# Strassen's scheme for the full down projections of a two-layer hybrid encoder

## What is computed

```
h = rmsnorm(x, g_ffn)
z = dwconv3(h @ w_up)                 # 1024 -> 5632 channels, centred convolution of width 3
x = x + (silu(z_gate) * z_val) @ w_down      # 2816 -> 1024 channels
```

## Time and profile before

| what | value |
|---|---|
| median of 3 runs | 1104.07 us (1103.85 to 1104.14) |
| profiled execution, span from first to last instruction | 1102.4 us |
| what lies around the span, against the median | 1.7 us |
| PE busy | 1092.6 us, 99% |
| PEld busy | 905.8 us, 82% |
| DVE / ACT / POOL busy | 531.0 / 484.7 / 464.8 us |
| granted TensorE clock | 0.999 of full speed |

### The profile page before, as it was taken

The page is one execution under the profiler, slowest core; times in us unless marked ns, Lnnn a source line. Parts: engine busy times, 40 slices in busy tenths (PEclk is TensorE's granted clock), DMA queues, the critical chain, the costliest instruction groups (busy, mean ns, idle before and its releaser), DMA issues.

```text
span 1102.4 us, 16315 instructions
## 1 busy us (share of the span) xinstructions
PE 1092.6 (99%) x5328; PEld 905.8 (82%) x5328; DVE 531.0 (48%) x816; ACT 484.7 (44%) x656; POOL 464.8 (42%) x202
## 2 busy tenths in 40 slices
PE   9999999999999999999999999999999999999997
PEld 7788888888888888888878888888888888888886
DVE  5726755655215551255536368456541355314545
ACT  7835444454225441344557344346432454313451
POOL 5334234344534443544634332435444444444450
PEclk9999999999999999999999999999999999999999
DMA  8222223232222222222522212222332322232222
GB/s 301 93 96 78 68 76 105 78 109 100 96 95 94 97 96 95 96 96 97 180 97 81 91 63 74 95 77 96 115 95 76 115 96 95 79 117 91 96 77 78
DMA packets 33607, 108.79 MB, mean 99 GB/s; under 512 B 3984, under 2 KB 6800, under 8 KB 33552
## 3 DMA queue, kind: packets, MB, share of 16 engines
q1 hardware_dynamic: 32848, 107.03, 29.2%
q10 hardware_dynamic: 704, 1.07, 0.3%
HBM read 105.98 MB, written 2.10 MB: 98 GB/s over the span
## 4 chain that ended last, share of the span: by engine, by line
PE 97%; DVE 1%; DMA 1%; ACT 0%; POOL 0%; SPq 0%; issue 0%; DVEq 0%
PE acc L1044 28%; PE acc L1045 28%; PE acc L1046 28%; PE acc L1170 3%; PE acc L1171 3%; PE acc L1172 3%; PE side L1140 1%; PE side L1258 1%; PE side L1242 1%; DMA x<-xT 1%; PE side L1248 1%; PE side L1221 1%; DVE arena L1019 1%; PE side L1201 1%; PE acc L1132 0%; PE acc L1121 0%
## 5 line engine op out<-in xcount | busy, mean ns | idle before, releaser
L339 POOL TENSOR_TENSOR w_lo<-w_raw,w_hi 128x1024 fp32r<-128x1024 f32 x188 | 453.4, 2416 | 600.6 <-ACT w_hi L348 600.6
L1044 PE MATMUL acc<-xg_hi,w_hi 128*128 128x512 f32 x864 | 338.8, 392 | 0.0
L1045 PE MATMUL acc<-xg_lo,w_hi 128*128 128x512 f32 x864 | 336.3, 389 | 0.0
L1046 PE MATMUL acc<-xg_hi,w_lo 128*128 128x512 f32 x864 | 336.2, 389 | 0.0
L348 ACT ACTIVATE w_hi<-w_raw 128x1024 fp32r<-128x1024 f32 x190 | 200.0, 1057 | 255.2 <-PE acc L1046 219.2
L1044 PEld LDWEIGHTS acc<-xg_hi,w_hi 128*128 128x128 f32 x864 | 162.2, 188 | 35.8 <-issue 2.0
L1046 PEld LDWEIGHTS acc<-xg_hi,w_lo 128*128 128x128 f32 x864 | 162.2, 188 | 33.9
L1045 PEld LDWEIGHTS acc<-xg_lo,w_hi 128*128 128x128 f32 x864 | 162.2, 188 | 33.5 <-issue 0.5
L1044 PE MATMUL acc<-feat_hi,w_hi 128*128 128x512 f32 (+1 forms) x492 | 188.9, 384 | 0.0
L1045 PE MATMUL acc<-feat_lo,w_hi 128*128 128x512 f32 (+1 forms) x492 | 188.8, 384 | 0.0
L1046 PE MATMUL acc<-feat_hi,w_lo 128*128 128x512 f32 (+1 forms) x492 | 188.8, 384 | 0.0
(11 more groups left out here) (131 smaller groups left out, 803.2 us busy)
## 6 DMA issues: line engine op xcount, KB each, us to landing
w_raw<-slabs SPq DMA_DIRECT2D x190, 512.0 KB, 3.3
outT<-arena SPq DMA_DIRECT2D x7, 256.0 KB, 2.3
ln_sb<-ln_gb SPq DMA_DIRECT2D x2, 512.0 KB, 7.7
w_raw<-slabs SPq DMA_DIRECT2D x4, 128.0 KB, 4.6
x<-xT ACTq DMA_DIRECT2D x2, 256.0 KB, 4.6
x<-xT SPq DMA_DIRECT2D x2, 256.0 KB, 5.9
x<-xT ACTq DMA_DIRECT2D x1, 512.0 KB, 7.2
w_raw<-slabs SPq DMA_DIRECT2D x2, 256.0 KB, 6.9
```

Of the source, the lines that this page charges most:

```text
L339: pool.tensor_tensor(w_lo[:, w], w_raw[:, w], w_hi[:, w].bitcast(F32), ALU.subtract).then_inc(lo_done, 1)
L1044: pe.matmul(out, wh, ah, start=first, stop=False)
L1045: pe.matmul(out, wh, al, start=False, stop=False)
L1046: return pe.matmul(out, wl, ah, start=False, stop=last)
```

## The change

In the full parts, each quad of four down slabs (eight input tiles, four output tiles) is computed as a 2x2 by 2x2 block product with seven unit products in place of eight. The blocks of the weights are output tiles even/odd by input tiles even/odd (four slabs `raw(0)` to `raw(3)`, arranged anew on the host by `quad_major`); the blocks of the features are even/odd tiles by first/second half of the tokens (`H = 256`). A unit is 24 matmuls of 256 columns for two output tiles side by side in one bank: 4 pairs x 2 output tiles x 3 products. Below, U1 to U7 are the seven units of the first quad of a part and V1 to V7 those of the second, in PE's order; U3 is made in two halves, U3a and U3b.

```diff
+                def unit(bank, slot_of, pairs, moving, first):
+                    for k in pairs:
+                        for r in range(2):
+                            a = slot_of * SLAB + r * (SLAB // 2) + k * P
+                            xh, xl = moving(k)
+                            out = acc[bank][:, r * H:(r + 1) * H]
+                            pe.matmul(out, w_hi[:, a:a + P], xh, start=(first and k == 0 and r == 0), stop=False,
+                                      skip_group_check=True)
+                            pe.matmul(out, w_hi[:, a:a + P], xl, start=False, stop=False, skip_group_check=True)
+                            last = pe.matmul(out, w_lo[:, a:a + P], xh, start=False, stop=(k == KP - 1),
+                                             skip_group_check=True)
+                    return last
...
+                    pe.wait_ge(lo_sum, 3 * (n // 2) + 1)
+                    pe.wait_ge(y_ready, ys + 1)
+                    pe.wait_ge(feat_ready, feats + KT - 1)
+                    unit(0, 0, every_pair, b11, True).then_inc(unit_done, 1)
+                    pe.wait_ge(lo_sum, 3 * (n // 2) + 2)
+                    pe.wait_ge(y_ready, ys + 2)
+                    pe.wait_ge(t_ready, stages + 2 * KP - 1)
+                    unit(1, 1, every_pair, t1, True).then_inc(unit_done, 1)
+                    pe.wait_ge(lo_sum, 3 * (n // 2) + 3)
+                    pe.wait_ge(y_ready, ys + 3)
+                    unit(2, 3, range(0, 2), b21, True)
+                    pe.wait_ge(lo_done, L * NS + slab + 1 + RING)
+                    pe.wait_ge(unit_added, 3 * n + 1)
+                    unit(0, 2, range(0, 3), t2, False)
+                    pe.wait_ge(t_ready, stages + 2 * KP)
+                    unit(0, 2, range(3, 4), t2, False).then_inc(unit_done, 1)
+                    pe.wait_ge(lo_done, L * NS + slab + 3 + RING)
+                    pe.wait_ge(unit_added, 3 * n + 2)
+                    pe.wait_ge(feat_ready, feats + KT)
+                    unit(1, 1, every_pair, b22, False).then_inc(unit_done, 1)
...
```

DVE, in the stages of the full parts: the sums of the features (T1 to T4, in the arena), and in the last stage of a part also the four sums of the weights of the first quad, between the steps of the stage:

```diff
+                    scale(0)
+                    taps(0, 0)
+                    if sums is not None:
+                        sums(1)
+                        sums(2)
+                    scale(1)
+                    taps(0, 1)
+                    gate(0)
+                    if sums is not None:
+                        sums(4)
+                        sums(3)
+                    scale(2)
+                    dve.wait_ge(feat_hi_done, L * NF + tile + (KT + 1))
+                    dve.tensor_tensor(lo(0, H), gated[0][:, 0:H], hi(0, H).bitcast(F32), ALU.subtract)...
+                    dve.wait_ge(even_copied, stage + 1)
+                    dve.tensor_tensor(t1, gated[0][:, H:S], even_copy, ALU.subtract).then_inc(t_done, 1)
+                    taps(1, 0)
+                    dve.wait_ge(t_hi_done, stage * 2 + 1)
+                    dve.tensor_tensor(lo(H, H), t1, hi(H, H).bitcast(F32), ALU.subtract).then_inc(t_ready, 1)
+                    scale(3)
+                    taps(1, 1)
+                    gate(1)
+                    ... t2, t3, t4 ...
+                    if added is not None:
+                        added()
+                    ... lo(S, S) of the odd tile, then t_lo[:, t_at] (768 columns) ...
...
+                            dve.tensor_tensor(sum_s1, raw(1), raw(3), ALU.add).then_inc(sum_done, 1)
...
+                    make = sums_of(part, 1)
+                    make(1)
+                    low(0, raw(0), 1)
+                    add_unit(0, 0, 0, 2, 7 * n + 6, x_done, 3 * n + 1)
+                    make(2)
+                    low(1, sum_s1, 2)
+                    make(4)
+                    make(3)
+                    add_unit(0, 1, 0, 0, 7 * n + 7, x_done)
+                    low(3, raw(2), 3)
+                    add_unit(1, 0, 0, 3, 7 * n + 8, unit_added)
```

Fourteen additions of 512 columns (`add_unit`) take the place of the eight of a part. ACT makes a high part for each of the seven weight operands (14 in place of 8 a part) and in each stage a copy of the even half, T1's high part and the 768 columns of T2 to T4; its list for the first quad is, behind all of the last stage:

```diff
+                    act.wait_ge(t_done, stage * 2 + 2)
+                    on_its_own(act)
+                    act.activation(odd, gated[1], ACT.Copy).then_inc(feat_hi_done, 1)
+                    act.activation(t_of, t_raw[:, H:4 * H], ACT.Copy).then_inc(t_hi_done, 1)
...
+                def last_units(n, slab):
+                    act.wait_ge(unit_done, 7 * n + 1)
+                    act.wait_ge(sum_done, 4 * n + 4)
+                    unit_hi(0, raw(1), hi_done)
+                    act.wait_ge(unit_done, 7 * n + 2)
+                    unit_hi(1, sum_s4, hi_done)
```

POOL makes all seven low parts of the first quad and four of the second; DVE makes the other three (`low` above):

```diff
+            def low_quad(L, part, g):
+                n, slab = quad_at(L, part, g)
+                if g == 0:
+                    pool.wait_ge(hi_sum, 3 * n + 1)
+                    low(0, raw(0)).then_inc(lo_sum, 1)
+                    pool.wait_ge(hi_sum, 3 * n + 2)
+                    low(1, sum_s1).then_inc(lo_sum, 1)
+                else:
+                    pool.wait_ge(lo_sum_vector, 3 * (n // 2) + 1)
+                pool.wait_ge(hi_done, L * NS + slab + 1)
+                pool.wait_ge(sum_done, 4 * n + 4)
+                low(2, sum_s2[:, :]).then_inc(lo_done, 1)
+                if g == 0:
+                    pool.wait_ge(hi_sum, 3 * n + 3)
+                    low(3, raw(2)).then_inc(lo_sum, 1)
+                pool.wait_ge(hi_done, L * NS + slab + 2)
+                low(0, raw(1)).then_inc(lo_done, 1)
+                if g:
+                    pool.wait_ge(lo_sum_vector, 3 * (n // 2) + 3)
+                pool.wait_ge(hi_done, L * NS + slab + 3)
+                low(1, sum_s4).then_inc(lo_done, 1)
+                pool.wait_ge(hi_done, L * NS + slab + 4)
+                low(2, raw(3)).then_inc(lo_done, 1)
```

More of the change, by code:

```diff
@@ L148, in encoder @@
         z = [slot(i) for i in range(4)]
+        sum_s1, sum_s4 = slot(4, 2), slot(6, 2)
+        t_raw, even_copy = slot(20, 2), slot(22)[:, 0:H]
         acc = [ctx.enter_context(nc.psum_tensor(f"acc{i}", [P, S], F32)) for i in range(RING)]
@@ L334, in _, with low_slabs @@
                                    ALU.subtract).then_inc(lo_done, 1)
[L335 to L340, removed]
+            def low_slabs(L, first, end):
+                with pool.Fori(L * (NS // RING) + first // RING, L * (NS // RING) + end // RING) as q:
+                    for j in range(RING):
+                        pool.wait_ge(hi_done, q * RING + (j + 1))
+                        low(j, raw(j)).then_inc(lo_done, 1)
@@ L343, in _ @@
+            for L in range(DEPTH):
+                before = RING if L == 0 else 0
+                for part in range(FULL_PARTS):
+                    low_slabs(L, before, N_FFN + part * PART + 2 * KT)
+                    for g in range(QUADS):
+                        low_quad(L, part, g)
+                    before = N_FFN + (part + 1) * PART
+                low_slabs(L, before, NS)
         @block.scalar
@@ new lines, in add_unit @@
+                def add_unit(g, i, half, bank, n_units, done, before=None):
+                    if before is not None:
+                        dve.wait_ge(unit_added, before)
+                    dve.wait_ge(unit_done, n_units)
+                    to = x[:, g * RING * S:(g + 1) * RING * S].rearrange("p (r i s) -> p r i s", r=2, i=2)
+                    to = to[:, :, i, half * H:(half + 1) * H]
+                    dve.tensor_tensor(to, to, acc[bank][:, :].rearrange("p (r s) -> p r s", r=2),
+                                      ALU.add).then_inc(done, 1)
@@ new lines, in part_of, with moving, t_part @@
+                def part_of(odd, half):
+                    def moving(k):
+                        w = slice(half * H, (half + 1) * H)
+                        return tuple(featT(hi, 2 * k + odd)[:, w] for hi in (True, False))
+                    return moving
+                def t_part(i):
+                    def moving(k):
+                        a = k * 3 * H + (i - 2) * H
+                        return t_hi[:, a:a + H], t_lo[:, a:a + H]
+                    return moving
+                b11, t1, b21, b22 = part_of(0, 0), part_of(0, 1), part_of(1, 0), part_of(1, 1)
@@ L1355, in _ @@
                     if part < FULL_PARTS:
-                        with pe.Fori(0, KT // RING) as q:
-                            for j in (1, 2, 3):
-                                down_tile(j, q, *places)
+                        down_quads(part)
                     else:
@@ L1428, in token_major, with quad_major @@
         return w[2 * s * P:2 * (s + 1) * P, col:col + S].reshape(2, P, S).transpose(1, 0, 2).reshape(P, SLAB)
+    def quad_major(w, rows, m):
+        v = w[rows.start:rows.stop, m * P:(m + RING) * P].reshape(KP, 2, P, 2, 2, P)
+        return [v[:, odd, :, :, i].transpose(1, 2, 0, 3).reshape(P, SLAB) for odd in range(2) for i in range(2)]
     A_W = B_W = 512
@@ L1447 @@
             rows = range(tiles.start * P, tiles.stop * P)
-            slabs += [channel_major(w_down[l], rows, m * P) for m in range(KT)]
+            if len(tiles) == KT:
+                for m in range(0, KT, RING):
```

(3 more changed lines are left out.)

234 lines of the change are left out of this document (214 added, 20 removed).

## The result

The kernel with the change takes 1158.15 us (median of 4 runs, 1155.0 to 1158.75) against 1104.07 before: a ratio of 1.0484, 95% interval 1.0469 to 1.0499. The profiled execution took 1158.42 us, its span is 1156.5, the mean granted clock 0.975 where it was 0.999. The forecast was 1149.6.

The account below looks back on a forecast made before the run. PE's matmul list was taken to bound the kernel; waits of 14.6 us a part less 3.2 saved give 11.4, 45.5 for four, so 1104.07 + 45.5 = 1149.6 us, range 1114 to 1168.

Parts of the forecast that it names:

- What the change removes: PE's matmul list: 168 matmuls of 256 columns replace 96 of 512, saving 3.2 us a part, 12.9 us over four.
- Rival 4: PE's smaller matmuls don't pay, with a pitch of 0.13 us between bank halves: 1163 us, chance 0.02.
- Durations: DVE costs: 1.22 us a sum of 1024 columns, 0.96 for 768 columns, 21.6 us an up stage.
- 4.7 us late: DVE's lateness when the last up stage begins, bounds 3.1 (no table loads) to 5.5; it was 0.6 before.
- the walk's 0: Time zero of the step-by-step reckoning of last stage and first quad: when PE ends the last up slab.
- U1 starts at 4.6: First quad: PE's first unit waits for late DVE and starts 4.6 us after the last up slab instead of 0.
- U2's 1.6 us: First quad: PE waits 1.6 us after U1's end, as T1's low part on DVE waits for POOL.
- A wait of 2.25: First quad: PE waits 2.25 us at U3a for POOL's low part of raw(2), ready at 14.15.
- U5's 3.65: First quad: PE waits 3.65 us, since ACT in order makes the difference's high part late and two POOL low parts follow.
- V3's 2.45: Second quad: PE waits 2.45 us for V1's addition, behind DVE's third low part, which waits for POOL.
- Rival 3: The clock falls to 1.2 GHz behind U5's and V3's waits: 21 us more, 1170 us, chance 0.12.
- Rival 1: Cover suffices: DVE's late stage is absent, PE stays the bound, waits under 3.2 us a part; 1091.2 us, chance 0.06.

Follow-up runs that it names:

- experiment 6: Against the kernel with the change: sums moved into DVE's gaps, second quad's DVE order changed, ScalarE's high part of the difference made early; 1095.71 us.
- experiment 5: Kernel with the change plus useless PE products filling the waits ahead of U1 (28 or 14) and U5 (12); 1157.47 us.
- experiment 4: Kernel with the change, DVE's order in the second quad altered: difference before S4, V1's addition before the third low part, S4 last; 1144.5 us.
- the kernel without sums: Kernel with the change, leaving out the four weight sums of each part's first quad, so part of the computation is missing; 1132.42 us.
- second kernel of experiment 1: Kernel with the change plus 12 useless PE products of 128 columns ahead of U5, half the first trial's number; 1157.73 us.
- Experiments 3: Against the kernel with the change: first quad's weight sums left out, 1132.42 us; or all kept but moved behind scales, with T1's low part later, 1124.93 us.
- experiment 6, without ScalarE's part: The kernel with all orders together, but ScalarE's high part of the difference put back behind that of T2 to T4; 1109.72 us.
- experiment 1: Kernel with the change plus useless PE products of 128 float32 columns ahead of U5: 24 gave 1164.91 us, 12 gave 1157.73 us.

## Why the prediction was right, and where it was not

The time fell within the range, and of the 54 us that were lost the waits are the larger part and the forecast one: PE waits for late DVE, POOL and ScalarE work in the four down stretches. The lower clock behind them was no part of the forecast's sum. Step by step:

- **What the change removes** held. The pitch is 0.12 us, and the ledger closes with the 12.9 us in both the kernel after and the one of experiment 6. Rival 4 is out.
- **Durations** held: sums 1.22 us, 768 columns 0.96 (taken at 0.96), DVE's stage 21.7 us (first scales at 246.38 and 268.11) where 21.6 was worked out.
- **"4.7 us late"** was one number for all parts and should have been two. In the first part of a layer DVE's last stage begins 9.1 us before the walk's 0, in the second 12.4, where the walk had 11.4. So "U1 starts at 4.6" became waits of 6.8 and 3.5 us (with the pitch), mean 5.15. What the walk left out in the first part is a late start: the first scale of the first stage there stands behind the norm's reciprocal (L834, 196.54 to 199.89) and comes 5.6 us after its bank, in the second part at once.

```profile
200.51 0.70 DVE L1102 TENSOR_TENSOR side<-acc,rstdT 128x512 f32<-128x512 f32 x1 [0.62 <-DVE rstdT L834]
```

Two numbers of the walk don't follow from its own terms: the lower bound of the lateness, 3.1 without the table loads, would be 3.0 less 0.4, 2.6; and the second and third scale, said to come "5 to 7 us behind their banks", are 6.8 and 8.8 behind them in the walk. They came 9.1 and 10.9 us behind in the first part, 5.7 and 7.7 in the second.

- **U2's 1.6 us** did not show, since U1 ran slow; with U1 at full clock it is there, 1.4 in the view and 1.6 as the ledger counts (experiment 5).
- **"A wait of 2.25" at U3a** was 1.0 to 2.05, **U5's 3.65** was 3.2 in three parts and 1.74 in one, **V3's 2.45** was 2.6. For V3 the port's part is in the trace: DVE's third low part took 3.13 us instead of 1.22.
- **The sum of waits** was put at 4 x 14.6 = 58.4 us and came to 49.4.
- **The term that I left out of the sum is the clock.** Rival 3 named it and put its fall behind U5 and V3, 21 us. It came in addition to the forecast, behind U1, U5 and once U3a, 18.1 us. The earlier trace rows had shown it for an idle stretch of 6.4 us, and I gave it 0.12 for want of a row with work behind a gap. The Trainium skill (TensorE: Matmul & The Clock Gate, HAM oscillation) has idle gaps between bursts halve the clock, and the trace of the kernel after agrees: 0.50 behind gaps of 3.2, 3.5 and 6.8 us. But such a gap does not always do it: behind one of 3.5 and one of 3.2 us in experiment 4, and two of 3.2 in the kernel without sums, the clock stayed full. The gap at V3 is 2.6 us and had no fall behind it in the kernel after, but four in the second kernel of experiment 1.

The waits' excess (-9.0) and the clock (+18.1) put the result 9 us over the forecast; the two errors are not independent, as experiment 5 shows: a part of the slow matmuls stands where a wait would have been. That the time lies so near the forecast is in this respect luck: the forecast waits with the clock on top would be 1167.7 us, just inside the range.

Rival 1 was argued away with "the ACT order alone gives U5 a wait of 3.3 us". Experiments 3 and 6 bear that out (3.1 us at U5 with the DVE waits of the first quad gone, and in 6 with V3's gone as well), and show that it was an order too: by moving instructions alone, the kernel comes within 4.5 us of rival 1's 1091.2. The orders are worth 33.2 (DVE's first quad and stages), 13.7 (second quad) and 8.7 us (ScalarE, with S4) each by itself, 55.6 added up, and 62.4 as a whole; the last wait that goes takes the clock's fall with it (ScalarE's step is worth 14.0 at the end: 1109.72 - 1095.71).

Open: what decides behind which of several gaps the clock falls, and for how long. The kernels show that it moves; they don't isolate the condition, and no kernel was profiled twice to tell what changes from one execution to the next. Open too is what T1's low part is worth by itself.

## What to carry to other kernels

Work added to an engine that is not the bound costs by its place: put it where that engine waits for another (here the 1.24 us behind each scale), and not between a finished bank and the operation that empties it. Where an in-order engine makes operands for two consumers, write its list by who needs what first, and don't make one earlier than needed if it takes a port from one that is due. When waits of a few microseconds appear on PE, count the lower clock behind them as a further term, but expect a part of it to be hidden by the next wait.

## What the runs showed of the hardware that was not expected

- One gap of 3.0 us a part, the only one of its down stretch, was followed by a clock of 0.5 in all four parts (experiment 6, without ScalarE's part); matmuls of 256 columns then come 0.213 us apart instead of 0.12. Yet gaps of 3.2 to 3.5 us had no fall behind them four times in two other kernels (experiments 3 and 4).
- How long the clock stays low is not fixed by the gap: behind the same 6.8 us it was 5.7 us in one kernel and 3.1 in another whose list is the same up to there. Where it was the shorter, a gap of 2.0 us (U3a) had a second fall behind it. The same gap of 2.0 us had none in the first and third part of the kernel without sums.
- POOL is held up by DVE as DVE is by POOL: its low part of 2.40 us took 3.37 where DVE's third low part, waiting since 318.30, went in ahead of it in the second quad (320.30 in the kernel after).
- A plain float32 product of 128 columns costs 0.22 us (24 in 5.28 us, experiment 1), nearly the 0.2268 of one with rounded operands and 512 columns.
